# Reordered loads at the start and between two layers of a decoder trunk: two adaLN units ahead of x's tiles, the latents' weights between the row tiles, the first latent transposes behind the second product

## What is computed

```python
cond = jax.nn.silu(c)
for i in range(DEPTH):
    mod = cond @ ada_w[i] + ada_b[i]
    sh_m, sc_m, g_m, sh_f, sc_f, g_f = jnp.split(mod, 6, axis=-1)
    h = modulate(rms_norm(x, norm_mix[i]), sh_m, sc_m)
    ...
    x = x + g_m[:, None, :] * y          # y: diff_attention(h) or mla_attention(h)
    h = modulate(rms_norm(x, norm_ffn[i]), sh_f, sc_f)
    x = x + g_f[:, None, :] * hier_moe(h, ...)
# mla_attention begins with
    lat = h @ w_in                       # 1024 x 672
    cq, ckv, k_pe = lat[..., :384], lat[..., 384:640], lat[..., 640:]
    q = rms_norm(cq) @ w_uq ; kv = rms_norm(ckv) @ w_ukv
```

## Time and profile before

| | us |
|---|---|
| runs of the kernel before, median of three | 1271.87 |
| lowest, highest | 1269.29, 1272.16 |
| the profiled execution, its own time | 1268.93 |
| its span | 1267.2 |
| TensorE busy in the span | 1036.8 |
| VectorE busy | 620.0 |
| ScalarE busy | 330.6 |
| GpSimd busy | 94.1 |

### The profile page before, as it was taken

One profiled execution on the slowest core, in us unless ns is written; L12 is line 12 of the kernel. 1 busy time (PEld: TensorE's weight loads), 2 busy tenths in 40 slices (PEclk: granted clock), 3 DMA queues, 4 the chain that ended last, 5 costly groups with the idle time before them and its releaser, 6 DMA issues.

```text
span 1267.2 us, 14783 instructions
## 1 busy us (share of the span) xinstructions
PE 1036.8 (82%) x5370; PEld 613.4 (48%) x5370; DVE 620.0 (49%) x1500; ACT 330.6 (26%) x913; POOL 94.1 (7%) x121
## 2 busy tenths in 40 slices
PE   2799999887992899877768899898993799877775
PEld 1344444554452565544435555555453556544443
DVE  5999699785337222222245377775236222221133
ACT  2311111775220211111123455565111111110110
POOL 1000000000000011111000000000000111111111
PEclk9999999997995899999999999999995799999998
DMA  9778777108634899999984300203325699999981
GB/s 376 288 290 316 308 295 302 64 2 332 249 126 176 338 420 419 420 419 420 409 329 185 115 1 19 82 1 133 150 81 234 264 417 419 419 419 420 418 363 72
DMA packets 63038, 332.96 MB, mean 263 GB/s; under 512 B 10543, under 2 KB 10799, under 8 KB 31600
## 3 DMA queue, kind: packets, MB, share of 16 engines
q1 hardware_dynamic: 46384, 289.29, 56.3%
q0 software_dynamic: 13824, 33.37, 6.9%
q10 hardware_dynamic: 2752, 9.28, 1.9%
HBM read 316.67 MB, written 32.52 MB: 276 GB/s over the span
## 4 chain that ended last, share of the span: by engine, by line
PE 48%; DMA 23%; DVE 18%; issue 4%; ACT 4%; SPq 3%; DVEq 0%; POOLq 0%; ACTq 0%
PE PP L611 9%; DMA AHS<-in_moe_w 7%; PE PP L676 7%; DMA RQK<-in_moe_w 7%; PE PP L691 5%; DMA ring<-in_moe_w 5%; PE PP L507 4%; SPq L431 3%; PE PP L766 3%; DVE AHS L1231 3%; PE PP L526 3%; DVE ring L1231 2%; PE PP L808 2%; PE PP L812 2%; PE PP L563 2%
## 5 line engine op out<-in xcount | busy, mean ns | idle before, releaser
L507 PE MATMUL PP<-ring,AHS 128*128 128x512 f32 x384 | 170.0, 599 | 9.3 <-ACT AHS L916 9.3
L1552 DVE TENSOR_TENSOR PS<-PS,PP 128x256 f32<-128x256 f32 x33 | 13.9, 421 | 235.9 <-PE PP L676 235.9
L507 PEld LDWEIGHTS PP<-ring,AHS 128*128 128x128 f32 x384 | 72.6, 193 | 94.8 <-issue 94.8
L611 PE MATMUL PP<-ring,AHS 128*128 128x512 f32 x256 | 113.1, 601 | 0.8 <-ACT AHS L1102 0.8
L676 PE MATMUL PP<-RQK,RV 128*64 128x256 f32 x768 | 91.2, 395 | 19.3 <-issue 15.7
L1562 DVE SCALAR_TENSOR_TENSOR PS<-PP,small,GF 128x512 f32<-128x512 f32 x66 | 46.5, 746 | 116.8 <-PE PP L691 116.8
L676 PEld LDWEIGHTS PP<-RQK,RV 128*64 128x64 f32 x768 | 66.3, 143 | 47.5 <-issue 31.4
L676 PE MATMUL PP<-ring,RV 128*64 128x256 f32 (+1 forms) x672 | 79.2, 380 | 11.4 <-issue 11.4
L676 PE MATMUL PP<-AHS,RV 128*64 128x256 f32 x640 | 72.5, 380 | 13.4 <-issue 13.4
L611 PEld LDWEIGHTS PP<-ring,AHS 128*128 128x128 f32 x256 | 48.9, 193 | 60.0 <-issue 60.0
L676 PEld LDWEIGHTS PP<-ring,RV 128*64 128x64 f32 (+1 forms) x672 | 60.3, 139 | 33.8 <-issue 20.4
(11 more groups left out here) (300 smaller groups left out, 1544.5 us busy)
## 6 DMA issues: line engine op xcount, KB each, us to landing
RQK<-in_moe_w SPq DMA_DIRECT2D x72, 1024.0 KB, 26.7
ring<-in_moe_w SPq DMA_DIRECT2D x63, 1024.0 KB, 27.3
AHS<-in_moe_w SPq DMA_DIRECT2D x60, 1024.0 KB, 28.9
ring<-in_ada_t SPq DMA_DIRECT2D x24, 1024.0 KB, 6.2
AHS<-in_ada_t SPq DMA_DIRECT2D x24, 1024.0 KB, 7.4
ring<-in_da_w_qkv SPq DMA_DIRECT2D x12, 1024.0 KB, 9.2
y_d<-GF POOLq DMA_DIRECT2D x2, 4096.0 KB, 29.3
AHS<-y_d ACTq DMA_DIRECT2D x8, 1024.0 KB, 13.2
```

The costliest lines, as they stand in the source:

```text
L507: last = mm(PB[n % 4][:, :], HT[:, c, t * P:(t + 1) * P], us[c // 4][:, (c % 4) * NH:(c % 4 + 1) * NH], start=c == 0, stop=c == C - 1)
L611: last = mm(PB[2 * t + n][:, :], (OT, OTM)[l][:, k, t * P:(t + 1) * P], us[k // 2][:, (k % 2) * D + n * NH:(k % 2) * D + (n + 1) * NH], st ...
```

## The change

Three loads and one step of TensorE change their place.

At the start SP issues two adaLN units first, then a tile of x ahead of each of the units 2 to 5. The tiles count on a semaphore of their own each (xl0 to xl3), and ScalarE's squares wait for their own tile. VectorE normalises tile t after unit t + 1, not after unit t.

At the join ScalarE issues the first two Y tiles only. SP waits for Y1, issues the three parts of w_in, then Y2 and Y3, then w_uq. In layer 1 ScalarE issues all four as before.

TensorE does turn_latents(0) after the second half of the second product, not between its halves.

The thresholds of the semaphores xl0 to xl3 rise by 16 where they are waited for later (lines 1354, 1391, 1909), and the stores of the result count on a semaphore "out".

```diff
@@ SP's queue @@
-            for t in range(T):
-                sp.dma_start(X[:, t, :], A["x"][0, t * P:(t + 1) * P, :]).then_inc(sem("x"), 16)
+            def load_x(src, t):
+
+                sp.dma_start(X[:, t, :], src[t * P:(t + 1) * P, :]).then_inc(sem(f"xl{t}"), 16)
 
             def stream(l):
                 for n, (src, k, slot, held) in enumerate(plan[l]):
+                    if l == 0 and 2 <= n < 2 + T:
+                        load_x(A["x"][0], n - 2)
                     if l == 1 and n == 0:
-                        sp.wait_ge(sem("xl0"), 16)
+                        sp.wait_ge(sem("xl1"), 32)
+                    if l == 1 and n == 3:
+                        for t in range(2, T):
+                            sp.dma_start(Y[t], y_rows[0][t]).then_inc(sem(f"xl{t}"), 16)
@@ TensorE, latents @@
                 def third_tile():
                     transpose_x(2, 2)
-                    turn_latents(0)
...
                 project(1, third_tile)
+                turn_latents(0)
                 project(2, fourth_tile)
@@ ScalarE, squares @@
                 if k == 0:
-                    act.wait_ge(sem("x"), 16 * T)
+                    act.wait_ge(sem(f"xl{t}"), 16)
@@ ScalarE, load_rows @@
-                for t in range(T):
+                for t in range(T if l else 2):
                     act.dma_start(Y[t], y_rows[l][t]).then_inc(sem(f"xl{t}"), 16)
@@ VectorE, add_row @@
-                dve.wait_ge(sem(f"xl{t}"), 16)
+                dve.wait_ge(sem(f"xl{t}"), 32)
                 link(tt(X[:, t], X[:, t], Y[t][:, k], ALU.add))
@@ VectorE, the order of its stages @@
             for u in range(AHEAD):
                 ada(u)
-                if u < T:
-                    normalise_x(0, u)
+                if 1 <= u <= T:
+                    normalise_x(0, u - 1)
```

More of the change, by code:

```diff
@@ L438, in _ @@
                     for t in range(T):
-                        sp.dma_start(X[:, t, :], x_d[t * P:(t + 1) * P, :]).then_inc(sem(f"xl{t}"), 16)
+                        load_x(x_d, t)
                 for n in range(PAIRS):
@@ L458, in _ @@
                 sp.wait_ge(sem("res"), 2 * T + t + 1)
-                sp.dma_start(out[t * P:(t + 1) * P, :], X[:, t, :]).then_inc(sem("x"), 16)
-            sp.wait_ge(sem("x"), 32 * T)
+                sp.dma_start(out[t * P:(t + 1) * P, :], X[:, t, :]).then_inc(sem("out"), 16)
+            sp.wait_ge(sem("out"), 16 * T)
         @block.tensor
@@ L1353, in residual @@
                 if l:
-                    dve.wait_ge(sem(f"xl{t}"), 32)
+                    dve.wait_ge(sem(f"xl{t}"), 48)
                 for n in range(2):
@@ L1908, in layer @@
                 for t in range(T if l else 0):
-                    pool.wait_ge(sem(f"xl{t}"), 48)
+                    pool.wait_ge(sem(f"xl{t}"), 64)
                     g.tensor_tensor(Y[t][:, 0], Y[t][:, 0], Y[t][:, 1], ALU.add).then_inc(sem("ysum"), 1)
```

## The result

| | before, us | after, us |
|---|---|---|
| median, six runs each | 1271.96 | 1259.88 |
| lowest, highest | 1268.64, 1274.40 | 1255.86, 1262.40 |
| the profiled execution | 1268.93 | 1255.86 |
| its span | 1267.2 | 1254.1 |

The changed kernel takes 0.9903 of the time before, with a 95% interval of 0.988 to 0.9927: 12.3 us less, 9.3 to 15.3. The forecast was 1259.1. Both profiled executions were short ones of their kernel, 3.0 and 4.0 us under its median.

The account below looks back on a forecast made before the run. It took VectorE, starting late behind x's loads, to bound the start, and TensorE's waits for w_in and modulation the join. Terms 3.4 + 3.4 + 2.5 + 3.5 = 12.8 us off the median 1271.87 gave 1259.1, range 1254 to 1266.

Parts of the forecast that it names:

- The start: First 40 us: with two adaLN units ahead of x, gains(0) comes 3.4 us earlier (2.5 to 4.0).
- The join's loads: Join of the layers: w_in ahead of Y2 and Y3 saves 3.4 us of TensorE's wait and 2.5 through its clock.
- the 1.3 for the copy of x: Join: w_in lands 1.3 us later if the 512 KB copy of x's first tile to DRAM is all served ahead.
- The wait's term: Join: the first latent product starts at 661.6 in place of 664.96, 3.4 us (0 if w_in is no earlier).
- The clock: First latent product's first half: a gap of only 1.6 us keeps TensorE's clock up, 2.5 us back (0 to 2.5).
- The first transposes: Join: moving turn_latents(0) behind the second product's second half removes a TensorE wait of 3.47 us, 3.5 us (or 3.0).
- clock: Rival at the join: the clock falls anyway or w_in comes about a microsecond late, 2.5 us less, 1261.6; chance 0.18.
- the start gives nothing: Rival at the start: the first product's weights are held up or ScalarE's roots stall VectorE, 1262.5; chance 0.10.
- w_in no sooner: Rival at the join: w_in comes no sooner and only the transposes' gain remains there, 1265.0; chance 0.06.
- doesn't show: Rival: the gain is taken back where expert weights stream, or the join waits elsewhere, 1271; chance 0.06.
- the slower one: Rival at start and join: loads on SP's queue share the engines and don't land in turn, 1284.2; chance 0.04.

Follow-up runs that it names:

- the start alone: Changed kernel with the join's loads and the latent transposes put back as before: 1269.52 us against 1272.79 for the kernel before, ratio 0.9971.
- the run with x behind everything: Changed kernel with x's four tiles issued behind all eight adaLN units and the first product's weights: 1278.61 us against 1271.99 for the kernel before, ratio 1.0053.
- the loads alone: Changed kernel with the start and the latent transposes put back, leaving the join's new load order: 1267.79 us against 1272.79 for the kernel before, ratio 0.9968.
- the join alone: Changed kernel with only the start put back, so the join's loads and transposes stay moved: 1262.75 us against 1272.79 for the kernel before, ratio 0.9933.
- the early w_in: Changed kernel with w_in issued right behind the last expert weights, not waiting for Y: 1258.5 us against 1272.32 for the kernel before, ratio 0.9901.
- the run with fills in four gaps: Changed kernel plus unread transposes before the mixes, behind layer 0's attention and before each layer's first expert: 1258.49 us against 1272.32 before, ratio 0.9898.
- the two other runs with fills: Changed kernel plus 22 unread transposes before the mixes: 1256.74 us, ratio 0.9879; the same with w_in right behind the expert weights: 1260.6 us, ratio 0.9902.

## Why the prediction was right, point by point

**The start** (forecast 3.4; the start alone measures 3.7, 2.4 to 5.0). Right, and by its steps: gains(0) at 35.08 for a reckoned 35.1, the idle 2.12 before the first normalisation for 1.7, the product at 37.02 for 36.9 to 37.3. One step was off without effect: the first unit waited for silu(c), not for its own landing, yet VectorE began at 8.78, before the reckoned 9.4. That the gain outlives da_project was argued from the earlier trace rows and is shown by the start alone, whose join begins 3.6 us earlier (639.5). The other traces bear it out: the join begins at 641.9 to 645.5 in the five executions with the old start, at 638.8 to 641.2 in the eight with the new one (the run with x behind everything left out).

**The join's loads** (3.4 for the wait, 2.5 for the clock). Right in mechanism, in the traces of the changed order: w_in in time or level with tile 0's modulation, Y2 and Y3 covered. Two steps were off without effect. Y1 landed at 647.9 and not at 646.7 (650.4 less the shift), and w_in still at 657.1 for a reckoned 657.0 (660.7 less the shift): the reckoned 4.8 + 4.1 us from Y1's landing on give 656.8, so hardly any of the 1.3 for the copy of x was needed. Y2 landed at 661.4 for a reckoned 659.5 and kept 1.5 us of cover. In other executions w_in is the later one, by a part of a microsecond (the loads alone, the second profile of the changed kernel). The wait's term was too large: the first latent product gained 5.73 - 3.68 = 2.05 us in the profiled pair, not 3.4. Of the missing 1.35, 1.1 are tile 0's chain, whose modulation ended at 658.98 and not at 661.53 - 3.68 = 657.85; most of that is the first mix at the lower clock, which VectorE could take 3.89 us after the mixes' start, 2.97 in the profile on which the forecast rests.

**The clock.** The size was right (7.70 to 5.40 in the profiled pair), the certainty was not. The step "with a gap of 1.6 us I expect no fall" held in the changed kernel's first profile, in the join alone, in the early w_in, in the run with x behind everything and in the run with fills in four gaps (5.40 after 1.86 to 1.88 us), and failed in the loads alone and the second profile (7.09 after 1.97 and 2.50) and in the two other runs with fills (8.33 and 7.09 after 1.85 and 1.86). So the length of the gap alone doesn't tell. Nor do the mixes before it: the four kernels without fills and with a gap of 1.86 all kept the clock, three behind mixes of 8.38 to 8.49 us and one, with x behind everything, behind mixes of 7.11; with fills (5.48, 7.11, 7.11) it was kept once in three. What decides it in each execution stays open. Nor was this term's reach foreseen: the 1.3 us after the latents, counted in no term, go with it.

**The first transposes** (forecast 3.5; alone 4.8, 3.2 to 6.5). The mechanism was right: the wait went, and no other took its place. This is the term that was mis-sized, on the evidence of the traces: the step that the earlier trace rows show 1.00 over the idle 3.4 us, so that the wait cost only itself, holds for the first profile alone. In the second profile of before, in the start alone and in the loads alone the same wait was followed by 11.3 to 11.4 us for 9.2 us of work, and the transposes themselves took 1.30 us, not 0.71. Where that happens the move is worth 3.47 + 2.2 + 0.6 = 6.3 us, an estimate from these rows, and the measured 4.8 lies between.

**The sum** came out at 12.3 for 12.8. Taken alone the join's loads gave 4.1 for 5.9, the transposes 4.8 for 3.5 and the start 3.7 for 3.4; each forecast lies at the edge of its interval or inside it, and the errors nearly cancel. That the sum came so close is in part luck: two terms were off by 1.3 and 1.8 us in opposite directions. Of the rivals, "clock" happened in part of the executions, "the start gives nothing", "w_in no sooner" and "doesn't show" are excluded by the parts alone, and the slower one by the landings. The steps of the clock elsewhere stayed under the 2 us that the prediction allowed them.

## What to carry to other kernels

Read a stage's idle time together with what runs behind it: a wait of TensorE is worth its length and, in some executions, the slower work after it, here 3.5 us of wait and up to 2.8 of work. When loads share one queue, count bytes in the order of issue and put each load by the moment of its first use; the reckoning held to about half a microsecond for moves of 3 and of 20 us at the start, and missed by 3.3 where Y and a copy of x were in flight at the join. One profiled execution is one draw: where a term hangs on TensorE's clock, take a second profile before giving it a size.

## What the runs showed of the hardware that was not expected

After an idle stretch of the same 3.4 to 3.5 us TensorE's granted clock was 1.00 in one execution of the same kernel and 0.50 in another, and after 1.86 us too both occurred, in different kernels (5.40 and 7.09 us for the same 16 records). The Trainium skill (TensorE: Matmul & The Clock Gate, What's actually happening) says that the number of slow matmuls at a kernel's start is run-variable; these rows show it in the middle of a kernel, worth 1 to 3 us at each place. And in 14 traces out of 14 one such place went with another some 60 us later: 7.09 us or more for those 16 records with 0.66 to 0.70 behind the latents, 5.40 with 1.00.

With twenty-two transposes in the gap of 3.4 us before the mixes these took 5.48 us in one execution and 7.11 in two, and began 1.3 us later in the first. Without them they took 7.11 in two executions (the first profile of before, x behind everything) and 8.16 to 8.49 in the other nine, so only the 5.48 lies outside what comes without them. What TensorE does between VectorE's last rows and the mixes, 2.0 us without the added transposes, is not seen in the trace.
